# Six norms between phases: the additions of squares to pairs and fours on GpSimd instead of VectorE

## What is computed

```python
def rms_norm(x, w):                      # first block
    y = xf * lax.rsqrt(jnp.mean(xf * xf, -1, keepdims=True) + RMS_EPS)
    return (y * w).astype(x.dtype)
...
def layer_norm(x, g, b):                 # second block
    mu = xf.mean(-1, keepdims=True)
    var = jnp.mean(jnp.square(xf - mu), -1, keepdims=True)
    return ((xf - mu) * lax.rsqrt(var + LN_EPS) * g + b).astype(x.dtype)
...
hs = hs + keep * rms_norm(mix, norm_w[i, 1])
f = conv_ffn(rms_norm(hs, norm_w[i, 2]), ...)
hs = hs + keep * rms_norm(f, norm_w[i, 3])
```

## Time and profile before

| | |
|---|---|
| median of 3 runs | 1508.42 us (1505.79 to 1509.04) |
| the profiled execution | 1506.74 us |
| its span, first to last instruction | 1504.9 us |
| TensorE busy | 1458.1 us, 97% |
| VectorE busy | 1028.0 us, 68% |
| ScalarE busy | 789.2 us, 52% |
| GpSimd busy | 283.3 us, 19% |
| mean granted TensorE clock | 0.993 |
| DMA engines busy, q1 | 46.0% |

### The profile page before, as it was taken

How to read it: one execution, slowest core, us unless ns; L and a number is a source line. 1 busy time by engine, 2 the same in 40 slices (tenths; PEclk the granted TensorE clock), 3 DMA queues, 4 the chain that set the end, 5 groups by cost and what they waited for, 6 DMA issues and landing times.

```text
span 1504.9 us, 32342 instructions
## 1 busy us (share of the span) xinstructions
PE 1458.1 (97%) x11625; PEld 1390.7 (92%) x11625; DVE 1028.0 (68%) x1742; ACT 789.2 (52%) x1380; POOL 283.3 (19%) x307
## 2 busy tenths in 40 slices
PE   6999999899999999999999999999999999999997
PEld 5996888698999999899999998999999989999997
DVE  4884676548888468457888557777664697776654
ACT  5554433436665356346666445554544567554443
POOL 0201202101555000000555100003330012033300
PEclk9998999999999999999999999999999999999999
DMA  5552132063555544333566554346555443365651
GB/s 195 184 179 70 43 100 80 6 193 99 186 185 177 178 130 143 124 98 114 180 195 184 191 158 150 121 148 202 191 181 184 148 136 113 130 211 181 189 183 57
DMA packets 61141, 222.54 MB, mean 148 GB/s; under 512 B 6784, under 2 KB 7808, under 8 KB 60672
## 3 DMA queue, kind: packets, MB, share of 16 engines
q1 hardware_dynamic: 60912, 220.17, 46.0%
q10 hardware_dynamic: 144, 1.18, 0.2%
HBM read 220.28 MB, written 1.05 MB: 147 GB/s over the span
## 4 chain that ended last, share of the span: by engine, by line
PE 82%; DVE 11%; ACT 4%; issue 2%; DMA 1%; DVEq 0%; ACTq 0%; SPq 0%
PE bank L419 22%; PE bank L420 22%; PE bank L421 22%; DVE wlo L397 2%; PE bank L1043 2%; PE bank L438 1%; PE bank L439 1%; PE bank L445 1%; ACT whi L392 1%; PE bank L1941 1%; PE bank L604 1%; DVE work L1614 1%; DVE work L1612 1%; DMA par<-params 1%; DVE hs_sb L660 1%
## 5 line engine op out<-in xcount | busy, mean ns | idle before, releaser
L397 DVE TENSOR_TENSOR wlo<-raw,whi 128x1024 fp32r<-128x1024 f32 x399 | 502.3, 1264 | 276.3 <-ACT whi L392 275.2
L419 PE MATMUL bank<-xs,whi 128*128 128x258 f32 (+2 forms) x1976 | 568.3, 288 | 6.0 <-DVE wlo L397 5.5
L392 ACT ACTIVATE whi<-raw 128x1024 fp32r<-128x1024 f32 x399 | 418.9, 1056 | 282.3 <-PE bank L421 265.7
L420 PE MATMUL bank<-xs,whi 128*128 128x258 f32 (+2 forms) x1976 | 562.9, 285 | 0.0
L421 PE MATMUL bank<-xs,wlo 128*128 128x258 f32 (+2 forms) x1976 | 560.6, 284 | 0.0
L419 PEld LDWEIGHTS bank<-xs,whi 128*128 128x128 f32 x1976 | 373.6, 189 | 11.4 <-issue 8.6
L421 PEld LDWEIGHTS bank<-xs,wlo 128*128 128x128 f32 x1976 | 374.3, 189 | 0.0
L420 PEld LDWEIGHTS bank<-xs,whi 128*128 128x128 f32 x1976 | 373.9, 189 | 0.4 <-issue 0.2
L419 PE MATMUL bank<-hf,whi 128*128 (+3 forms) x1024 | 290.7, 284 | 0.5 <-DVE cv L754 0.5
L420 PE MATMUL bank<-hf,whi 128*128 (+3 forms) x1024 | 289.6, 283 | 0.0
L421 PE MATMUL bank<-hf,wlo 128*128 (+3 forms) x1024 | 289.6, 283 | 0.0
(11 more groups left out here) (470 smaller groups left out, 1538.8 us busy)
## 6 DMA issues: line engine op xcount, KB each, us to landing
raw<-stream SPq DMA_DIRECT2D x412, 512.0 KB, 3.7
con<-consts SPq DMA_DIRECT2D x1, 1284.5 KB, 7.7
big<-mla ACTq DMA_DIRECT2D x1, 1152.0 KB, 8.0
hs_sb<-hs SPq DMA_DIRECT2D x1, 1088.0 KB, 5.0
y_out<-hs_sb SPq DMA_DIRECT2D x8, 128.0 KB, 2.0
par<-params SPq DMA_DIRECT2D x1, 644.0 KB, 8.8
```

Source lines behind the costliest of these rows:

```text
L392: nc.scalar.activation(whi[:, s, :], raw[:, s, :], ACT.Copy).then_inc(hi_split, 1)
L397: nc.vector.tensor_tensor(wlo[:, s, :], raw[:, s, :], whi[:, s, :].bitcast(F32), ALU.subtract).then_inc(block_split, 1)
L419: nc.tensor.matmul(out_, whi[:, slot, w], hi, start=start, stop=False)
L420: nc.tensor.matmul(out_, whi[:, slot, w], lo, start=False, stop=False)
```

## The change

The functions `pair_sum` and `four_sum` go. A function `sums_pool` makes the same four pairs and two fours of a norm on GpSimd, each as soon as ScalarE's square is there, and TensorE's sums wait for GpSimd's marks. GpSimd's list has a call of it at each of the six places.

```diff
-    def pair_sum(dve, name, m, T, lo=0):
-
-        v = S("norm", "dve")
-        dve.wait_ge(*S("norm", "act").at(f"{name}_{m}"))
-        nc.vector.tensor_tensor(sq[:, m, lo:T], sq[:, m - 1, lo:T], sq[:, m, lo:T], ALU.add).then_inc(*v.mark(f"{name}_pair{m}"))
-
-    def four_sum(dve, name, m, T, lo=0):
-        v = S("norm", "dve")
-        if m % 4 == 3:
-            dve.wait_ge(*v.at(f"{name}_pair{m}"))
-            nc.vector.tensor_tensor(sq[:, m, lo:T], sq[:, m - 2, lo:T], sq[:, m, lo:T], ALU.add).then_inc(*v.mark(f"{name}_four{m}"))
+    def sums_pool(pool, name, T, lo=0):
+        v = S("norm", "pool")
+        for m in range(1, KC, 2):
+            pool.wait_ge(*S("norm", "act").at(f"{name}_{m}"))
+            nc.gpsimd.tensor_tensor(sq[:, m, lo:T], sq[:, m - 1, lo:T], sq[:, m, lo:T], ALU.add).then_inc(*v.mark(f"{name}_pair{m}"))
+            if m % 4 == 3:
+                pool.wait_ge(*v.at(f"{name}_pair{m}"))
+                nc.gpsimd.tensor_tensor(sq[:, m, lo:T], sq[:, m - 2, lo:T], sq[:, m, lo:T], ALU.add).then_inc(*v.mark(f"{name}_four{m}"))
+        pool.wait_ge(*v.at(f"{name}_four{KC - 1}"))
...
-            return "dve", f"{name}_four{m}", sq[:, m, lo:T]
+            return "pool", f"{name}_four{m}", sq[:, m, lo:T]
...
-            if m % 2 == 0 and m:
-                pair_sum(dve, name, m - 1, T1, t.start)
-            if m == 5:
-                four_sum(dve, name, 3, T1, t.start)
         lo(KC - 1)
-        pair_sum(dve, name, KC - 1, T1, t.start)
-        four_sum(dve, name, KC - 1, T1, t.start)
         split_lo(dve, fourth(phase))
...
         gdn_pool(pool)
+        sums_pool(pool, "pre1", T1, PRE_FIRST["pre1"])
         ffn_pool(pool, 0, G["up0"])
+        sums_pool(pool, "pre2", T1, PRE_FIRST["pre2"])
         ml_pool(pool)
+        sums_pool(pool, "pre3", T1, PRE_FIRST["pre3"])
         ffn_pool(pool, 1, G["up1"])
+        sums_pool(pool, "ln0v", T2)
         ffn_pool(pool, 2, G["up2"])
+        sums_pool(pool, "ln1v", T2)
         odd_pool(pool)
+        sums_pool(pool, "ln2v", T2)
         ffn_pool(pool, 3, G["up3"])
```

More of the change, by code:

```diff
@@ L2207, in ln_dve @@
                 lo(m - 1)
[L2208 to L2211, removed]
         if phase:
             lo(KC - 1)
-        if phase:
-            pair_sum(dve, name + "v", KC - 1, T2)
-            four_sum(dve, name + "v", KC - 1, T2)
         if phase:
```

## The result

| | before | changed |
|---|---|---|
| median, 9 runs each | 1507.85 us | 1512.6 us (1509.87 to 1517.42) |
| ratio | | 1.0041 (95% interval 1.0031 to 1.0051) |
| once more, 30 and 11 runs | 1507.07 us | 1511.44 us, ratio 1.0026 (1.0016 to 1.0036) |

The change makes the kernel slower, by the ratio 6.2 us in the first comparison and 3.9 in the second; the medians lie 4.75 and 4.37 us apart. The forecast was +7.5 and 1515.9, with 1511.0 to 1520.5 as its range: the median is inside that range, and the forecast size was over the measured one.

What follows compares the result with a forecast made beforehand. TensorE was taken to bound the kernel, VectorE counting only where TensorE waits for it. Pre norms 6.3 us plus ln norms 1.2 us gave +7.5 us, a median of 1515.9 us, range 1511.0 to 1520.5.

Steps and rivals of the forecast that it cites:

- the time of a pre norm is that of its last four-sum: In pre1, pre2 and pre3, a delay of the last four-sum delays the norm: 2.1 us each, 6.3 in all.
- The port's price: A GpSimd addition ahead of a VectorE instruction with two SBUF inputs costs VectorE 0.57 us and saves 0.35.
- The tail: Behind slice 7's residual, the fourth block's split precedes GpSimd's pair and four: 2.60 us to the four's end, 0.83 before.
- the case given at 1.8 us: GpSimd gets the port first, the split lies between pair and four, and a pre norm's last sum comes 1.8 us late.
- The ln norms: In ln0, ln1 and ln2 TensorE stops 0.4 us each for the last four, bounds 0 and 1.0, 1.2 us in all.
- The slack of 0.92 us: In ln0 before the change, the last four is ready 0.92 us before TensorE needs it.
- the forecast's own case: The main forecast of +7.5 us, chance 0.60, its own range from 1513.2 to 1520.4 us.
- the half-hidden case: Rival: later waits absorb TensorE's stops or the chain behind the logarithm has slack; +3.5 us, 1511.9 us, chance 0.16.
- No exclusion: Rival: VectorE and GpSimd do not exclude each other on these additions; -2.3 us in all, 1506.1 us, chance 0.08.
- A port held for the whole addition: Rival: VectorE waits out all of GpSimd's 0.76 us per addition; 12 us in all, 1520.4 us, chance 0.10.
- The lower clock: Rival: a pre norm's new hole of some 2 us lowers TensorE's clock; three times 3.4 us on top, 1526.1, chance 0.06.
- The signs: Expected profile marks: GpSimd additions of 0.8 to 1.9 us, residuals over 1 us, pre1's sum 2.6 us behind slice 7's residual.

Runs made afterwards that it cites:

- the last experiment: Kernel before, pre norms: GpSimd makes the four of slices 0 to 3, VectorE adds the last squares one after the other; ratio 0.9984, 1505.21 us.
- the additions and memsets beside VectorE: Two kernels, each the kernel before plus six GpSimd instructions per norm whose results nobody reads; ratio 1.0086 with additions, 0.9997 with memsets.
- the hole filled: Changed kernel plus twelve matmuls with unread results ahead of the last sum of each pre norm; ratios 1.0041 and 1.0045 to the kernel before.

## Why the prediction was right, and where it was off

- **That the time of a pre norm is that of its last four-sum** held: 5.4 of the 5.6 us are there, ScalarE starts its logarithm 1.7 us later in pre1, TensorE's later waits do not shrink, and an earlier sum (the last experiment) shortens the kernel. That TensorE has to wait anyway behind the wave was read in pre1; it holds in pre3 and not in pre2, where the stop at the sum counts by itself.
- **The port's price, 0.57 us per early addition that meets a two-input instruction**: measured 0.52 at the residuals and 0.58 at the split. Which three of four would meet one was right; slice 7's residual moved by 0.2 where 0.3 was forecast (pre3: 0.5, see the last section).
- **The tail, 2.1 us per pre norm: here is the step that was off.** The prediction put the split just ahead of GpSimd's pair, two instructions due within some hundredths. GpSimd came 0.05 us first, so the split stood between pair and four, the case given at 1.8 us. From the residual's end to the four's end that case comes to 2.33 us by the prediction's terms (-0.08 + 0.57 + 1.14 + 0.70), and 2.34 was measured. With the residual 0.2 late instead of 0.3 it measured 1.69.
- **The ln norms, 0.4 us each**: 0.06, by the same error. The pair undisturbed, the four ended at 1011.66, just when TensorE arrived. The slack of 0.92 us was rightly read. These two corrections take 1.9 us off the 7.5, which leaves the traces' 5.6. The measured median, 1512.6, lies under the 1513.2 at which the forecast's own case began; that it stayed in the stated range is owed to the part taken in for the half-hidden case, while the 5.6 us of the traces lie in the forecast's own range.
- **The rivals.** No exclusion fell with the additions and memsets beside VectorE. Its price of -2.3 us was too large besides: TensorE waited only 0.6 us for the fours before, and in the last experiment a four 0.48 us earlier brought the sum only 0.23 us forward. A port held for the whole addition fell with the residuals of 1.02 us. Half hidden fell in the traces, by the shifts that last from wave to wave; by its time alone the second comparison, 3.9 us, would fit it (3.5). The lower clock came in 2 of 20 runs, at 4.8 us where the rival gave 10.2, and filling the hole that the rival named did not prevent it. Both runs stand in the first comparison, among nine, and may be part of its 6.2 us.
- **The signs.** Additions of 0.8 to 1.9 us came, but the longest is the last four (1.62) and not the pair of slice 7, which follows from the order on the port. The last sum of pre1 stands 2.4 us behind slice 7's residual, where 2.6 was given. TensorE waits 1.5 us three times instead of some 2, and not in the ln norms. The clock in the profiled run was not as before (0.988).
- What the prediction lacked altogether is that the low stretches of the clock differ from run to run and from kernel to kernel. Two profiles of the same changed kernel differ by 1.4 us through one stretch and by 4.8 through three more. A sum of rows taken from one profile has that error, however exact the rows.

## What to carry to other kernels

Before an addition is given to GpSimd, list what VectorE does just then. In these rows it was free beside an instruction that reads a bank (0.49 us), and beside one with two inputs in SBUF it cost VectorE 0.52 us to save 0.35. Above all look at the first long VectorE instruction behind the last of a chain of GpSimd instructions, since it gets between them; either make it wait, which left 0.8 us of the 1.7 in the trace here, or keep the chain's end on VectorE. And where an engine is the last arrival, shorten what stands behind its last input (one addition instead of two) rather than what stands ahead.

## What was not expected of the hardware

- Two instructions 0.05 us apart decide who holds the port for 1.14 us: 357.59 against 357.64 here. An estimate from rows could not call that order. It was no accident of one run: in all six norms GpSimd comes first by 0.05 to 0.06 us, and so it does in the other profiles with the last two additions on GpSimd and no wait ahead of the split.
- In pre3 of the changed kernel VectorE stands idle for 0.29 us ahead of slice 7's addition to `hs`, and the profile shows nothing that it waits for:

```profile
711.20 0.06 DVE L659 MEMSET head_v<- 128x1 f32 x1
711.56 0.43 DVE L660 TENSOR_TENSOR hs_sb<-hs_sb,y 128x258 f32<-128x258 f32 x1 [0.29 <-issue]
```

The same 0.3 us are there in the second profile of the changed kernel, in both with the hole filled and in the one with pre norms alone (slice 7's residual 0.5 us late each time), and not where the split waits or the early additions alone are on GpSimd (0.15). It makes pre3's 2.0 us out of 1.7. The cause was not tried.
